# Stick-breaking scores: one four-byte product a head, or three products of rounded query and key parts

## What is computed

```python
def stick_breaking_attention(q, k, v):
    ...
        z = jnp.einsum('bqhd,bkhd->bhqk', q_blk, k, preferred_element_type=jnp.float32) * scale
        earlier = key_pos[None, :] < q_pos[:, None]
        log_keep = jnp.where(earlier, jax.nn.log_sigmoid(-z), 0.0)
        log_after = lax.cumsum(log_keep, axis=3, reverse=True) - log_keep
        weight = jnp.where(earlier, jnp.exp(jax.nn.log_sigmoid(z) + log_after), 0.0)
        return jnp.einsum('bhqk,bkhd->bqhd', weight.astype(v.dtype), v)
```

## Time and profile before

| | |
|---|---|
| three runs | 2234.18 us median (2232.79 to 2234.29) |
| the profiled execution's own time | 2232.53 us |
| its span in the trace | 2230.8 us |
| PE busy | 2191.7 us, 98% of the span |
| DVE busy | 1387.1 us, 62% |
| ACT busy | 798.7 us, 36% |

### The profile page before, as it was taken

The page is one execution under the profiler, slowest core; times in us unless marked ns, Lnnn a source line. Parts: engine busy times, 40 slices in busy tenths (PEclk is TensorE's granted clock), DMA queues, the critical chain, the costliest instruction groups (busy, mean ns, idle before and its releaser), DMA issues.

```text
span 2230.8 us, 28390 instructions
## 1 busy us (share of the span) xinstructions
PE 2191.7 (98%) x10128; PEld 1730.1 (78%) x10128; DVE 1387.1 (62%) x2101; ACT 798.7 (36%) x1166; POOL 0.2 (0%) x4
## 2 busy tenths in 40 slices
PE   7999999999999999999999999999999999999998
PEld 5777678888886666788888877777788878888886
DVE  5666664554447888655554466587855557888743
ACT  4555432222224555322222224447623223222222
POOL 0000000000000000000000000000000000000000
PEclk9999999999999999999999999999999999999999
DMA  4111133333332112233333332222233332333332
GB/s 130 50 56 57 51 101 100 97 94 93 100 91 67 57 56 66 76 94 95 102 95 95 94 78 71 63 67 67 57 107 96 94 99 85 104 94 94 99 94 90
DMA packets 368644, 188.31 MB, mean 84 GB/s; under 512 B 8969, under 2 KB 368314, under 8 KB 368570
## 3 DMA queue, kind: packets, MB, share of 16 engines
q1 hardware_dynamic: 368569, 187.30, 29.4%
HBM read 185.18 MB, written 2.10 MB: 84 GB/s over the span
## 4 chain that ended last, share of the span: by engine, by line
PE 88%; DVE 6%; ACT 3%; issue 2%; DVEq 0%; ACTq 0%
PE lin L1707 77%; PE S L1770 1%; PE ob L1801 1%; PE S L1783 1%; PE S L1868 1%; PE ob L1897 1%; DVE conv L1365 1%; ACT w_hi L531 1%; PE lin L1735 1%; DVE w_lo L918 1%; PE misc L1881 1%; PE S L1788 1%; ACT L798 0%; PE S L2025 0%; PE ob L2053 0%
## 5 line engine op out<-in xcount | busy, mean ns | idle before, releaser
L531 ACT ACTIVATE w_hi<-raw 128x1024 fp32r<-128x1024 f32 x361 | 381.4, 1057 | 850.0 <-PE lin L1707 823.6
L918 DVE TENSOR_TENSOR w_lo<-raw,w_hi 128x1024 fp32r<-128x1024 f32 x361 | 440.8, 1221 | 203.4 <-ACT w_hi L531 202.5
L1707 PE MATMUL lin<-h_hi,w_hi 128*128 128x512 f32 x1928 | 498.0, 400 | 3.5 <-DVE exact L1597 2.9
L1707 PE MATMUL lin<-h_lo,w_hi 128*128 128x512 f32 x1928 | 482.0, 392 | 0.0
L1707 PE MATMUL lin<-h_hi,w_lo 128*128 128x512 f32 x1928 | 478.4, 390 | 0.0
L1707 PEld LDWEIGHTS lin<-h_hi,w_hi 128*128 128x128 f32 x1928 | 360.6, 189 | 92.7 <-issue 15.1
L1707 PEld LDWEIGHTS lin<-h_hi,w_lo 128*128 128x128 f32 x1928 | 360.9, 188 | 74.8 <-issue 0.5
L1707 PEld LDWEIGHTS lin<-h_lo,w_hi 128*128 128x128 f32 x1928 | 359.5, 188 | 74.3 <-issue 0.5
L1707 PE MATMUL lin<-gu_hi,w_lo 128*128 128x512 f32 x528 | 131.4, 389 | 0.0
L1707 PE MATMUL lin<-gu_lo,w_hi 128*128 128x512 f32 x528 | 131.4, 389 | 0.0
L1707 PE MATMUL lin<-gu_hi,w_hi 128*128 128x512 f32 x528 | 131.4, 389 | 0.0
(11 more groups left out here) (362 smaller groups left out, 2182.3 us busy)
## 6 DMA issues: line engine op xcount, KB each, us to landing
raw<-in_w_in_dram SPq DMA_DIRECT2D x108, 512.0 KB, 3.7
raw<-in_w_gate_dram SPq DMA_DIRECT2D x44, 512.0 KB, 3.7
raw<-in_w_up_dram SPq DMA_DIRECT2D x44, 512.0 KB, 3.7
raw<-in_ffn_up_dram SPq DMA_DIRECT2D x44, 512.0 KB, 3.7
raw<-in_w_down_dram SPq DMA_DIRECT2D x32, 512.0 KB, 3.7
raw<-in_w_out_dram SPq DMA_DIRECT2D x24, 512.0 KB, 3.7
raw<-in_ffn_down_dram SPq DMA_DIRECT2D x16, 512.0 KB, 3.7
raw<-in_w_down_dram SPq DMA_DIRECT2D x16, 384.0 KB, 3.4
```

Source lines behind the costliest of these rows:

```text
L531: act.activation(w_hi[u.slot][:, :, :], raw[u.slot][:, :, :], ACT.Copy).then_inc(hi_ready, 1)
L918: dve.tensor_tensor(w_lo[u.slot][:, :, :], raw[u.slot][:, :, :], w_hi[u.slot][:, :, :].bitcast(f32), ALU.subtract).then_inc(lo_ready, 1)
L1707: ins = pe.matmul(acc, (wh, wh, wl)[part][:, k, :], (hi, lo, hi)[part][:, k0 + k, :], start=first and part == 0 and k == 0, stop=last and ...
```

## The change

Queries and keys of the stick-breaking attention are split like the weights and activations of the linear layers. DVE writes q and k to one buffer each (`q_full`, `k_full`, which are the two buffers of `qb`), ACT rounds each (`rounded`: `q_hi`, `k_hi`), DVE subtracts (`remainder`: `q_lo`, `k_lo`), and PE adds three matmuls a head, k_hi by q_hi, k_hi by q_lo, k_lo by q_hi, the two heads in turn, instead of one four-byte matmul. The score stage now waits for both remainders (`sb_lo`) instead of for k (`evac`).

```diff
--- before.py
+++ after.py
@@ -228,6 +228,7 @@
         o_lo = new("o_lo", [P, KT, SEQ], f32r)
         qb = [new(f"qb{s}", [P, SEQ]) for s in range(2)]
         kb = [new(f"kb{s}", [P, SEQ]) for s in range(2)]
+        q_full, k_full = qb[0], qb[1]
         vf = new("vf", [P, SEQ])
         vt = [new(f"vt{s}", [P, NB, P]) for s in range(2)]
         mix0 = 32 * 1024 + 14 * 1024
@@ -238,6 +239,9 @@
         soft_hi = new("soft_hi", [P, 2, sum(SPAN)], f32r)
         soft_lo = new("soft_lo", [P, 2, sum(SPAN)], f32r)
         wgt = new("wgt", [P, 2, sum(SPAN)])
+        q_lo, k_hi, k_lo = ([new(f"{k}{s}", [P, SEQ], f32r) for s in range(2)] for k in ("q_lo", "k_hi", "k_lo"))
+        new = place(36 * 1024)
+        q_hi = [new(f"q_hi{s}", [P, SEQ], f32r) for s in range(2)]
         new = place(mix0)
         q_raw = [new(f"q_raw{j}", [P, SEQ]) for j in range(2)]
         q_sq, q_rs, q_n, q_c = (new(f"q_{k}", [P, SEQ]) for k in ("sq", "rs", "n", "c"))
@@ -359,6 +363,7 @@
 
 
         sb_z, sb_soft_t, sb_soft, sb_exp_in = sem("sb_z"), sem("sb_soft_t"), sem("sb_soft"), sem("sb_exp_in")
+        sb_hi, sb_lo = sem("sb_hi"), sem("sb_lo")
         sb_w, sb_pv, sb_vtr, sb_vt, sb_o = sem("sb_w"), sem("sb_pv"), sem("sb_vtr"), sem("sb_vt"), sem("sb_o")
 
 
@@ -558,7 +563,7 @@
                 act.activation(lam_sum[:, :], lam_sum[:, :], ACT.Exp).then_inc(prep_act, 1)
                 act.activation(cols[32:48, C_A:C_A + 1], cols[32:48, C_A:C_A + 1], ACT.Exp).then_inc(prep_act, 1)
 
-            def stick_breaking(u0):
+            def stick_breaking(u0, v0):
                 def soften(n, g):
 
                     t, j = n.scale(4) + g, NB - 1 - g
@@ -569,6 +574,10 @@
                     act.activation(soft_j, soft_j, ACT.Exp, scale=-1.0).then_inc(sb_soft_t, 1)
                     act.wait_ge(sb_soft_t, t.of(3, 2))
                     act.activation(soft_j, soft_j, ACT.Ln, bias=1.0).then_inc(sb_soft_t, 1)
+
+                def rounded(n, j):
+                    act.wait_ge(evac, n.of(3, v0 + j + 1 + CREDIT))
+                    act.activation((q_hi, k_hi)[j][n.slot][:, :], (q_full, k_full)[j][:, :], ACT.Copy).then_inc(sb_hi, 1)
 
                 def weights(n, g):
                     t, j = n.scale(4) + g, NB - 1 - g
@@ -587,6 +596,8 @@
                         hi(At(U_WO[0] + 2))
                     else:
                         hi(u + 2)
+                        rounded(n + 1, 0)
+                        rounded(n + 1, 1)
                     soften(n, 3)
                     weights(n, 2)
                     if not last:
@@ -596,6 +607,8 @@
                 hi(At(u0 + 2))
                 rotary_and_exps()
                 hi(At(u0 + 3))
+                rounded(At(0), 0)
+                rounded(At(0), 1)
                 soften(At(0), 0)
                 by_two(act, KT, pair)
 
@@ -866,7 +879,7 @@
             token_scale(0)
             for l in range(min(until, 2)):
                 if l == 0:
-                    stick_breaking(U_QKV[l])
+                    stick_breaking(U_QKV[l], V_QKV[l])
                 else:
                     differential(U_QKV[l], V_QKV[l])
                 residual_begun(U_WO[l], V_WO[l], R_WO[l])
@@ -1001,9 +1014,14 @@
 
                     v = n.scale(3) + (v0 + j)
                     leave(v, n.scale(3) + (u0 + j))
-                    dst = (qb[n.slot], kb[n.slot], vf)[j]
+                    dst = (q_full, k_full, vf)[j]
                     dve.scalar_tensor_tensor(dst[:, :], lin[v.slot][:, :], 0.125 if j == 0 else 1.0, rsB[:, :],
                                              ALU.mult, ALU.mult).then_inc(evac, 1)
+
+                def remainder(n, j):
+                    dve.wait_ge(sb_hi, n.of(2, j + 1))
+                    dve.tensor_tensor((q_lo, k_lo)[j][n.slot][:, :], (q_full, k_full)[j][:, :],
+                                      (q_hi, k_hi)[j][n.slot][:, :].bitcast(f32), ALU.subtract).then_inc(sb_lo, 1)
 
                 def values(n):
                     dve.wait_ge(sb_vtr, n.of(1, 1))
@@ -1047,6 +1065,8 @@
                         qkv_tile(n + 1, 0)
                         split(u + 2)
                         qkv_tile(n + 1, 1)
+                        remainder(n + 1, 0)
+                        remainder(n + 1, 1)
                     softplus(n, 3)
                     if not last:
                         split(u + 3)
@@ -1062,6 +1082,8 @@
                 qkv_tile(At(0), 0)
                 split(At(u0 + 2))
                 qkv_tile(At(0), 1)
+                remainder(At(0), 0)
+                remainder(At(0), 1)
                 softplus(At(0), 0)
                 qkv_tile(At(0), 2)
                 values(At(0))
@@ -1763,12 +1785,13 @@
                 def scores(n, g):
 
                     j = NB - 1 - g
-                    pe.wait_ge(evac, n.of(3, v0 + 2 + CREDIT))
+                    pe.wait_ge(sb_lo, n.of(2, 2))
                     pe.wait_ge(sb_w, (n.scale(4) + g).of(1, 1))
-                    for a in range(2):
-                        k = slice(64 * a, 64 * a + 64)
-                        pe.matmul(S2[g % 2][:, a, 0:SPAN[j]], kb[n.slot][k, P * j:P * j + P], qb[n.slot][k, P * j:SEQ],
-                                  start=True, stop=True)
+                    for part, (k_part, q_part) in enumerate(((k_hi, q_hi), (k_hi, q_lo), (k_lo, q_hi))):
+                        for a in range(2):
+                            k = slice(64 * a, 64 * a + 64)
+                            pe.matmul(S2[g % 2][:, a, 0:SPAN[j]], k_part[n.slot][k, P * j:P * j + P], q_part[n.slot][k, P * j:SEQ],
+                                      start=part == 0, stop=True, skip_group_check=part > 0)
                     for a in range(2):
                         ins = pe.matmul(S2[g % 2][:, a, 0:P], mask("ident"), mask("hide_sb"), start=False, stop=True,
                                         skip_group_check=True)
```

## The result

| | median | runs |
|---|---|---|
| before | 2233.48 us (2232.38 to 2234.29) | 4 |
| with the change | 2260.89 us (2256.75 to 2263.08) | 4 |

The ratio is 1.0121, with a 95% interval from 1.0108 to 1.0134: the change costs 27 us, 1.2%. It also spreads: the four runs lie 6.3 us apart, those of before 1.9. The profiled execution took 2260.20 us, and 2232.53 before, so the two traces differ by 27.7 us.

A forecast was written before the change was run, and what follows sets the result against it. TensorE, busy 98% of the span, was taken as the bound. Softening 19.0, first pair 2.1, scores -2.7 and clock 3.5 sum to +21.9 us on the profiled 2232.53, giving a median of 2256 us, range 2248 to 2265.

The forecast's parts named there:

- The held softening: Per pair preparing a next one, ACT softens group 3 only after rounding k; exponents(3) 2.72 us later, seven times, +19.0 us.
- T: Moment the next pair's key projection's last product row lets DVE write k; exponents(3) began at T + 6.16 before the change.
- The tie of the two branches: DVE's softplus of group 3 (+2.72 us) and ACT's weights of group 2 (+2.57) delay PE alike; one wait ahead of weigh(2).
- The first pair: PE's first scores wait for q and k roundings and k_lo behind ACT's w_hi: 40.77 instead of 38.67, +2.1 us.
- the later wait: PE's 2.47 us wait for DVE's table work, ending at 47.94; forecast not to absorb the first pair's delay.
- The score products: Three rounded steps replace the four-byte score matmul; the three long groups save 0.16, 0.12 and 0.06 us, -2.7 over eight pairs.
- The rival with exposed loads: Weight loads of the score steps not overlapped with matmuls: 4.4 us above the forecast, 2260 us; chance 0.07.
- The clock: TensorE falls to half clock behind some new waits, 1.4 us each, 2.5 more than before: +3.5 us, bounds 0 to +9.8.
- the covered stall: Rival: the chain to exponents(3) stays under 6.16 us from the key tile, so no stall; 2233.6 us, chance 0.05.
- The stall without falls: Rival: PE's seven waits come but leave the clock alone; 18.4 us, 2252.6 us, chance 0.22.
- a fall at every pair: Rival: a half-clock stretch behind each of the seven waits; 18.4 + 9.8 us, 2262 us, chance 0.10.
- The likeliest case: The forecast itself: stall at seven pairs with some clock falls, 2254 to 2260 us, chance 0.53.

The follow-up runs named there:

- e1: The changed kernel, with ACT rounding k behind the softening of group 3 instead of ahead of it: 2235.04 us, ratio to before 1.0007.
- e2: The kernel before, with only one wait added: ACT waits for the next pair's key tile ahead of softening group 3; 2252.09 us, ratio 1.0083.
- e3: The kernel before, with three rounded score matmuls a head, remainders left out and no added work elsewhere: 2232.17 us, ratio 0.9992.
- e4: The changed kernel, with ten rounded 512-column matmuls of constants filling PE's wait ahead of weigh(2) in seven pairs: 2251.70 us.
- e7_head_by_head: The changed kernel with k rounded behind group 3's softening, first-pair roundings ahead of the weight tile, and each head's three score products issued together: 2232.86 us.
- e6_table_wait: The changed kernel with k rounded behind group 3's softening, first-pair roundings ahead of the weight tile, and ten constant matmuls in PE's table wait: 2232.52 us.

## Why the prediction was right, and where it was off

The forecast was 2256 us within 2248 to 2265; measured 2260.9. Its steps, one by one:

- **The held softening**: right. 7 x 2.72 us was forecast for T to exponents(3), 7 x 2.59 measured (8.74 against 6.15): 18.1 us instead of 19.0. The tie of the two branches was right to 0.2 us: PE waited 2.23 us ahead of weigh(2), and in the three pairs without a half-clock stretch a little more ahead of exponents(3). There the weight load waited for soft_lo:

```profile
PEld S L1806 <- DVE soft_lo L1046: 1.5, 3, 0.5
```

  For PE this is some 0.2 us of the 0.5: at T = 130.32 exponents(3) stands at 139.06, 2.16 us behind the start of the product row ahead of it (136.90), and before the change the same distance was 99.63 - 97.69 = 1.94. So DVE's branch ended last, by a little; in the pair shown above, at half the clock, PE came later than soft_lo. The wait ahead of weigh(2) was 0.3 us shorter than the 2.57 forecast, since an activation begins 0.1 us before the one ahead of it ends (99.54 + 0.63 against 100.08, 102.21 + 1.06 against 103.17), which I hadn't taken off; ACT's branch has both of these overlaps and DVE's only the first. e1 and e2 show from both sides that the order on ACT is the cause, and not the work.
- **The first pair**: 2.1 forecast, 1.9 measured, not absorbed by the later wait, as forecast.
- **The score products**: stages of 0.99, 0.82, 0.67 and 0.64 us forecast; 0.99, 0.81, 0.68 and 0.58 measured. 2.7 us forecast, 0.29 to 0.33 a pair measured, 2.3 to 2.6. The weights of the second product load while the first streams over the same rows. In e1's trace the load of q_lo's product begins at 91.34, and the q_hi matmul ahead of it lasts from 91.23 to 91.73:

```profile
91.23 0.50 PE L1794 MATMUL S<-q_hi,k_hi 64*128 64x512 f32 x2
91.34 0.19 PEld L1794 LDWEIGHTS S<-q_lo,k_hi 64*128 64x128 f32 x2
91.57 0.39 PE L1794 MATMUL S<-q_lo,k_hi 64*128 64x512 f32 x2
```

  The Trainium skill, "TensorE: Matmul & The Clock Gate", Part 3 (Packing small matmuls), says in one sentence that a load overlaps matmuls in flight only where the row group differs; another sentence of the same part lets a load into a background weight buffer go ahead of them. The load at 91.34 overlaps on its own row group, against the first sentence and in keeping with the second. The rival with exposed loads falls, in e3 by its time as well: its slowest run took 2233.57 us, against 2236.5.
- **The clock**: the term that was mis-sized. I took 2.5 half-clock stretches more than before at 1.4 us each, +3.5. The stage got six more (units of 3.3 us), at four of the seven waits and at the table wait, two of them double; I hadn't thought of double ones. Their price can be read directly. From T to the next T the two pairs without a stretch take 30.23 us (about 30.3 was forecast), and the four with one take 31.50, 32.94, 31.42 and 31.46: 6.4 us for five units, 1.3 each. The sixth, at the table wait, lies between the first two key tiles, 31.53 us apart against 28.58: less the 1.9 of the first pair's wait, plus the 0.3 that the scores saved, 1.35. That is 7.7 us. As a remainder it is 8.1: exponents(3) of the last pair came 25.5 us later than before against the first key tile, less 18.1 and 1.9, and plus the 2.6 that the products saved. So the price of one was nearly right and their number wrong. e4 removes five of them and gives 9.2 us back by the medians, 7.9 by the profiled executions (2260.20 and 2252.33). Of these 7.9, 6.1 are there at the last exponents(3) (284.48 against 290.57), and 1.6 come across a stretch at 711.7 us which e4's profile doesn't have. Why four of the seven waits were followed by a fall, and which ones, the runs don't settle. Behind the stage the trace has two more, at 1623.1 and 2247.7, in parts of the program that the change doesn't touch, and 2.1 us more of lateness:

```profile
1623.10:1626.30 3.20, 3.20 (x22) 2.58 (x19) 2.13 (x4) 2.12 (x3) 0.00 (x0) 0.50 0.37 88
2247.70:2251.00 3.30, 3.30 (x16) 3.30 (x17) 3.30 (x6) 1.64 (x3) 0.00 (x0) 0.50 0.00 0
```

  Why they fell there is open; other runs here have stretches near both places too (e3_scores_only at 1595 and 2220 us), the kernel before had none in its one profile. That profile is of an execution with a mean granted clock of 0.997, and the executions of the same kernel beside the experiments read from 0.995 to 0.997, so such stretches come and go without any change. That these 2.1 us are a cost of the change isn't shown.
- **The rivals**: the covered stall fell (PE waits, seven times). The stall without falls, 2252.6, is what e4 shows, 2251.7. Of the single times that the rivals gave, 2260 for exposed weight loads came nearest and 2262 for a fall at every pair next, neither by its mechanism: the loads weren't exposed, and three of seven pairs had no fall. The likeliest case's own 2254 to 2260 was missed by 0.9 us. The clock came out 4.6 us above its term, and the softening, the first pair and the scores together 1.0 us below theirs. The range held because it allowed for a fall at every pair; it had no place for double ones, nor for falls behind the stage, and that these still fitted was luck.

The sum, as measured in the traces: 18.1 + 1.9 - 2.6 + 8.1 + 2.1 = 27.6 us, against 27.7 between the profiled executions. The 8.1 is itself a remainder, so this sum checks only the last term; with the 7.7 read directly it is 27.2.

## What to carry to other kernels

On an engine that works strictly in order, an added instruction costs what it waits for, not what it lasts: place it by the time at which its input is there, and look at which finished work would stand behind it. Read from the trace the margin of each thing that the bounding engine needs, here 0.9 and 1.35 us, before adding a wait upstream of it. Where TensorE is the bound, count more for a wait than its length, since the clock may fall with it, and expect the runs to spread: here waits of 2.23 us cost 3.1 each on average (five units of 1.3 us over seven waits), and in e2_wait_only waits of 1.79 us about 2.5.

## What the runs showed that I had not expected

- Matmuls on different halves of the array's rows kept no order between them: in e7_head_by_head the second head's first product, fourth in the program, starts together with the first head's first, ahead of the two between. Issuing the heads in turn gains nothing.
- Half-clock stretches can be twice as long (6.7 us at 49.5 and 165.6), though PE was busy in 6.55 of the 6.7 us of the second. Both began 0.4 and 0.2 us before the wait was over (at 49.89 and 165.75); in e2_wait_only one that began 0.2 us before the table wait's end had the usual length, so what makes one double stays open.
- Useless matmuls in a wait paid: 70 of them took the time down by 9.2 us in e4_filled_wait. In e6_table_wait, ten in a single wait moved the stage 1.46 us ahead but not the median.
